# Attention and product-key feed-forward in float32 pairs, one core: GpSimd makes the odd v tile's low part beside dots

## The reference

```python
def block(xb):
    ...
    s_top, i_top = lax.top_k(s, PEER_TOPK)
    ...
    best, pos = lax.top_k(cand, PEER_TOPK)
    eidx = jnp.take_along_axis(cand_idx, pos, axis=-1)
    g = jax.nn.softmax(best, axis=-1)
    ug = jnp.take(u, eidx, axis=0)
    vg = jnp.take(v, eidx, axis=0)
    h = jax.nn.gelu(jnp.einsum('td,thkd->thk', xb, ug).astype(jnp.float32), approximate=False)
    return jnp.einsum('thk,thkd->td', (g * h).astype(x.dtype), vg)
```

## Time and profile before

| | |
|---|---|
| median of 3 runs | 1775.45 us (1773.05 to 1778.77) |
| the profiled execution, its own time | 1774.55 us |
| its span | 1772.4 us |
| mean granted TensorE clock | 0.983 |
| TensorE busy | 1700.3 us, 96% |
| VectorE busy | 1262.4 us, 71% |
| ScalarE busy | 639.2 us, 36% |
| GpSimd busy | 605.3 us, 34% |
| DMA | 422.76 MB, mean 239 GB/s |

### The profile page before, as it was taken

One profiled execution on the slowest core, in us unless ns is written; L12 is line 12 of the kernel. 1 busy time (PEld: TensorE's weight loads), 2 busy tenths in 40 slices (PEclk: granted clock), 3 DMA queues, 4 the chain that ended last, 5 costly groups with the idle time before them and its releaser, 6 DMA issues.

```text
span 1772.4 us, 23346 instructions
## 1 busy us (share of the span) xinstructions
PE 1700.3 (96%) x8969; PEld 1492.6 (84%) x8969; DVE 1262.4 (71%) x2325; ACT 639.2 (36%) x1011; POOL 605.3 (34%) x270
## 2 busy tenths in 40 slices
PE   8999998899979999999999999997999999999997
PEld 6898896677768899999999999996777777778775
DVE  1003345555259995998899999957888898888886
ACT  3213333443232234334344435432333343333333
POOL 4423221225353463444344433432232232322202
PEclk9999999999989999999999999998999999999999
DMA  5422101112312267777798999999999999999981
GB/s 190 172 81 72 48 24 50 48 60 83 143 48 96 84 179 276 240 246 280 255 335 323 333 345 335 348 365 376 373 376 372 380 376 377 367 382 379 385 278 60
DMA packets 144382, 422.76 MB, mean 239 GB/s; under 512 B 11152, under 2 KB 76944, under 8 KB 123024
## 3 DMA queue, kind: packets, MB, share of 16 engines
q1 hardware_dynamic: 125840, 287.05, 45.3%
q0 software_dynamic: 18432, 134.23, 20.2%
HBM read 368.80 MB, written 52.43 MB: 238 GB/s over the span
## 4 chain that ended last, share of the span: by engine, by line
PE 62%; DVE 24%; DMA 10%; issue 2%; ACT 1%; POOL 1%; SPq 0%; POOLq 0%; ACTq 0%; DVEq 0%
PE bank L1156 18%; PE bank L1157 18%; PE bank L1158 18%; DMA raw<-in_uv 7%; DVE acc L1066 6%; DVE wlo L1044 6%; DVE uvb L1052 4%; PE bank L1377 2%; DVE alo L1096 2%; DVE af L1089 2%; PE bank L1245 1%; PE bank L1212 1%; PE xpair L1260 1%; DMA gl<-g_scratch 1%; PE bank L1214 1%
## 5 line engine op out<-in xcount | busy, mean ns | idle before, releaser
L1156 PE MATMUL bank<-xhi,whi 128*128 128x384 f32 (+1 forms) x1440 | 516.2, 358 | 12.1 <-DVE xlo L796 8.5
L1157 PE MATMUL bank<-xlo,whi 128*128 128x384 f32 (+1 forms) x1440 | 509.4, 354 | 0.0
L1158 PE MATMUL bank<-xhi,wlo 128*128 128x384 f32 (+1 forms) x1440 | 508.9, 353 | 0.0
L539 POOL DMA_INDIRECT uvb<-in_uv,eidx x128 | 214.0, 1672 | 391.2 <-DVE acc L1066 371.0
L709 ACT ACTIVATE whi<-raw 128x1024 fp32r<-128x1024 f32 x256 | 270.0, 1055 | 207.6 <-DMA raw<-in_uv 135.4
L1156 PE MATMUL bank<-whi,ahi 128*128 128x512 f32 x768 | 305.9, 398 | 20.4 <-DVE alo L1096 20.4
L1157 PE MATMUL bank<-wlo,ahi 128*128 128x512 f32 x768 | 304.3, 396 | 0.0
L1158 PE MATMUL bank<-whi,alo 128*128 128x512 f32 x768 | 304.2, 396 | 0.0
L1156 PEld LDWEIGHTS bank<-xhi,whi 128*128 128x128 f32 x1440 | 273.5, 190 | 30.3 <-issue 12.0
L495 POOL TENSOR_TENSOR wlo<-raw,whi 128x2048 fp32r<-128x2048 f32 (+1 forms) x38 | 170.0, 4475 | 358.2 <-ACT whi L569 358.1
L1158 PEld LDWEIGHTS bank<-xhi,wlo 128*128 128x128 f32 x1440 | 273.2, 190 | 17.8
(11 more groups left out here) (191 smaller groups left out, 1870.6 us busy)
## 6 DMA issues: line engine op xcount, KB each, us to landing
raw<-in_u SPq DMA_DIRECT2D x128, 512.0 KB, 6.0
raw<-in_uv SPq DMA_DIRECT2D x128, 512.0 KB, 8.9
h_scratch<-hout SPq DMA_DIRECT2D x128, 192.0 KB, 6.3
g_scratch<-stage SPq DMA_DIRECT2D x48, 512.0 KB, 7.9
hl<-h_scratch SPq DMA_DIRECT2D x32, 768.0 KB, 10.3
gl<-g_scratch SPq DMA_DIRECT2D x32, 768.0 KB, 12.3
raw<-in_w_in SPq DMA_DIRECT2D x22, 1024.0 KB, 4.8
raw<-in_w_q SPq DMA_DIRECT2D x8, 1024.0 KB, 4.7
```

The lines of the kernel that those rows point to most:

```text
L539: nc.gpsimd.indirect_dma_start(out=uvb[:, k % UVB, :], out_offset=None, in_=a["uv"][:, :], in_offset=bass.IndirectOffsetOnAxis(ap=eidx[:, ...
L1156: mm(out, lh, rh, start=first, stop=False)
L1157: mm(out, lh, rl, start=False, stop=False)
L1158: return mm(out, ll, rh, start=False, stop=last)
```

## The change

In the 40 dot beats of the v stage the low part of the odd tile is made by GpSimd (line L553 of the new kernel), and VectorE leaves it out. GpSimd does not start when the high part is there but waits also until the second product of that beat is done (`a_done`, counted up by `product`), which in VectorE's order is the instruction before the first dot. The low parts of odd v tiles are now counted by two semaphores, one for GpSimd's and one for VectorE's, and `wait_low` chooses for TensorE and SyncE which to wait on. The wait of VectorE on GpSimd's count at tile 129 is dropped.

```diff
+def low_beside_dots(n):
+
+    return n % 2 == 1 and NT <= n < 2 * NT - 2 and n // 2 in SUM_BEATS
+
+
+def odd_lows(n):
+
+    pool = NT // 2 + sum(low_beside_dots(m) for m in range(NT + 1, n + 1, 2))
+    return pool, (n + 1) // 2 - pool
...
+        lo_odd = sem("lo_odd")
...
+        def wait_low(engine, n):
+
+            if n < NT or n % 2 == 0:
+                engine.wait_ge(tile_lo[n % 2], n // 2 + 1)
+            elif low_beside_dots(n):
+                engine.wait_ge(tile_lo[1], odd_lows(n)[0])
+            else:
+                engine.wait_ge(lo_odd, odd_lows(n)[1])
...
                 if n >= 4:
-                    sp.wait_ge(tile_lo[n % 2], (n - 4) // 2 + 1)
+                    wait_low(sp, n - 4)
...
             for n in range(2 * NT):
-                if n < POOL_ONLY or n < NT and n % 2 == 1:
+                if low_beside_dots(n):
+                    pool.wait_ge(a_done, n - NT + 3)
+                if n < POOL_ONLY or n < NT and n % 2 == 1 or low_beside_dots(n):
                     tile_low(n)
...
-                if n == NT + 1:
-                    dve.wait_ge(tile_lo[1], NT // 2)
                 V.tensor_tensor(wlo4[:, slot4(n), :], raw4[:, slot4(n), :], whi4[:, slot4(n), :].bitcast(F32),
-                                ALU.subtract).then_inc(tile_lo[n % 2], 1)
+                                ALU.subtract).then_inc(tile_lo[n % 2] if n < NT or n % 2 == 0 else lo_odd, 1)
...
                 tile_low(2 * beat)
-                if beat >= U_BEATS:
+                if beat >= U_BEATS and not low_beside_dots(2 * beat + 1):
                     tile_low(2 * beat + 1)
...
             for t in range(NT - 4):
-                pe.wait_ge(tile_lo[t % 2], (NT + t) // 2 + 1)
+                wait_low(pe, NT + t)
```

## The result

| | median us | range | runs | ratio to before [95% interval] |
|---|---|---|---|---|
| before | 1774.35 | 1773.05 to 1778.77 | 4 | |
| after | 1806.83 | 1804.14 to 1810.45 | 4 | 1.0177 [1.0153, 1.0201] |

The change costs 32 us. The forecast was a gain of 12: wrong, and the time lies outside the range. A ratio is estimated from the single runs and is not quite the quotient of the medians, here 1.0183. One run of the kernel before, of 1882.21 us at a granted clock of 0.842 where the others had 0.974 and more, is left out of every ratio.

A forecast was written before the change was run, and what follows sets the result against it. The v stage was taken as bound by a loop of raw load, ScalarE and VectorE; -1.1 - 2.0 - 9.5 = -12.6 us from 1774.55 gives 1762.0, plus 0.9 for the median: 1763, range 1758 to 1776.

The forecast's parts named there:

- What bounds the kernel: v stage: loop of raw load, ScalarE and VectorE, 51.6 us per six beats, falling to 49.0, below TensorE's 50.3.
- the 4 named as the sign of it: Sign the forecast is right: TensorE's waits on alo after the first total under 4 us.
- the 9.5 us that were priced as VectorE's time: v stage: TensorE stalls after the first pause won back by the shorter loop, 9.5 us taken from 0 to 13.
- Four gathers in a row: Rival, 12%, v stage: raw load waits behind four gathers, hl and gl; period 54.6 in half the periods, 1786 us.
- S + 9.7: Issue time of the next beat's even raw load, the one in the chain, 9.7 us after a dot beat's start S.
- The step on gathers: v stage: gathers queue behind GpSimd's new low part; 0 to 3 us of wait per three beats, taken as 0.
- a landing of 14.6: v stage: the critical raw load may take 14.6 us rather than 13.3 before TensorE stops setting the pace.
- The spacing: v stage: four gathers follow two lows, 2.17 us apart, from S + 5.7 to S + 14.4 of the second dot beat.
- The port: Dot beats: GpSimd's low sticks out past the dots and delays VectorE, 0.2 us per beat, ends 0 and 2.0.
- The start: Before the first v tile: one low fewer ahead, 1.1 us, and the gather of 1186.45 moved later, 2.0 us.
- The DMA engines: Rival, 17%: DMA bounds six beats at 51.3 us at 378 GB/s, so only the start is won, 1772.3 us.
- The port rival: Rival, 3%: lows start the dots late, sums pay 2.0 us instead of 0.2, loop 56.2 us, 1815 us.

The follow-up runs named there:

- e9: The change plus one wait: the second dot beat's gathers wait for the plain beat's products, so gathers leave late but in twos; 1762.17 us.
- e1: The change with GpSimd issuing a dot beat's two gathers ahead of the next dot beat's low part, not behind it; 1761.59 us.
- e7: The kernel before, all low parts on VectorE, with gathers held until the dots and the second pair until the plain beat's products; 1768.01 us.
- e6: e1 without the wait on a_done, so GpSimd makes the low part as soon as the high part is there; 1764.49 us.
- e2: The kernel before, no low part moved, with GpSimd waiting for each dot beat's dots before going on to the gathers; 1810.92 us.
- e8: e1 with the last two gathers of the u stage held until the first product of the v stage is done; 1761.99 us.
- e5: The change without its wait on a_done, gathers still behind the low part; 1798.41 us.

## Why the prediction was wrong

**What bounds the kernel: the loop right, its price not shown.** The raw load, then ScalarE, then VectorE's queue was the loop of the kernel before. With the gathers apart the time came out near the forecast of 1763: e9, which is the change and one wait, took 1762.17, and e1 1761.59. In e9 TensorE's later waits on alo were 3.2 us (8.7 - 5.5), under the 4 named as the sign of it, and the chain ran through TensorE's lines; in e1 they were 5.4. But e7, with every low part on VectorE, was already 7.5 us below before (1775.54 - 1768.01), and its ratio, 0.9956, cannot be told from that of e9, 0.9945. And e6 was faster than before with VectorE busier, 97% of this stretch instead of 87% (before, then e6):

```profile
1450.00:1700.00 250.00, 245.73 (x1051) 197.25 (x1050) 218.18 (x311) 89.18 (x138) 69.70 (x37) 1.00 1.01 377
1450.00:1700.00 250.00, 249.52 (x1066) 199.74 (x1066) 243.49 (x297) 90.30 (x137) 107.77 (x57) 1.00 1.01 375
```

So no run shows the 9.5 us that were priced as VectorE's time. The new spacing of the gathers can be the larger part of the gain of 12, and that the fast kernels lie at the forecast is partly luck.

**The step that failed** stands under "Four gathers in a row": "the load issued at S + 9.7 lands at S + 22.9, a landing of 13.2, as today". It took the 6.81 MB ahead of that load and divided by 396 GB/s, the rate of full engines. But the rate does not say who is served, and the engines were not full: they stood at a share of 0.49 for 8 us while four gathers were held, and the bytes that they did not move then had to pass later. The held low part ended at 1514.53 (1512.12 + 2.41) and the load of 1522.05 landed at 1538.15, 23.6 us behind it, where the step had 17.2. That load took 16.10 us, beyond the 15.9 from which that rival was said to decide. The step on gathers priced the crowd at 0 to 3 us of VectorE's waits for gathers; those came to 4.5 us in the whole stage. The price was paid by another: the raw loads in the other queue.

**The rival named the mechanism and sized it at half.** 1786 was worked out from one long load per 51.6 us, a period of 54.6 in half of the periods. The chain shows about two long loads, because each of the two pairs of dot beats in six beats sends its four, and the eight periods measured all took over 54 us, 55.1 on the mean. And no term was there for the clock, which gave 11 us after longer pauses. Its chance, 12%, was also too low: the rows of order already showed two low parts followed by four gathers through the whole stage. The slack of 1.4 us between a landing of 14.6 and one of 13.2 was the only thing between forecast and rival, and 13.2 was an assumption.

**The spacing was wrong.** Four gathers 2.17 us apart were assumed, from 1495.93 and 1498.10, though the gather of 1186.45 there took 0.94 us to issue; three of the four took 0.95 to 1.02, so they left 1.3 apart and the crowd was denser. What makes a gather take 0.95 or 1.9 us to issue was not tried.

**The port: priced at 0.2 per dot beat, measured 0.** The low part of 1488.93 ended at 1491.35, just ahead of the small product, whose mean from 1206 to 1700 us stayed at 161 ns, so the 0.3 us named as a sign did not come; the sums stayed at 1285 ns each. The order and place of the low part were as predicted.

**The start: right.** Forecast 1.1 + 2.0 us off the first pause of 9.6; after has 7.0, 2.6 less. In e2, where no low part moved but the gather of 1186.45 came later too, it was 7.5, so 2.1 us go with the gather. In e6, where again a third gather left among the first loads, it was 9.1, and in e8, with the last two gathers held as well, 1.8. Kernels with the same two gathers ahead of the loads had 5.3 to 7.5, so none of these is exact.

**The other rivals.** The DMA engines are no bound at 378 GB/s: e1 and e8 moved 389 over 460 us. The port rival did not come in the change; without the hold it did, in e5 and at alo in e6.

**Left open.** Whether the 8 us of idle engines ahead of the fours or the crowd behind them costs more: no kernel here had the one without the other.

## What to carry to other kernels

A compute step put ahead of DMA issues in an in-order queue is also a gate on them: ask not only whether they come in time, but in what groups they leave, and whose transfers they meet. A mean rate says nothing about the landing of one load; look at what the queues hold in the 10 us after its issue. Where pauses of TensorE grow from 1 us to 2 or more, price the clock with them as a risk. And a forecast that a repaired kernel then meets is not yet shown: a control with the repair and without the change (e7 here) can be almost as fast.

## What the runs showed that was not expected

- Holding four gathers together instead of two and two costs 43 to 45 us (e7 against e2, e9 against the change), with the same bytes and the same instructions.
- TensorE's clock fell after some short pauses of its work and not after others: after one of 1.79 us (ended 1487.59) the next stretch of 4 us stayed at 1.00, after one of 1.81 (ended 1653.20) it had 0.71, and after one of 3.64 the 8 us that followed had 0.68 and 0.89. The length alone does not decide: in e5 the 4 us behind pauses of 2.94 (ended 1544.41) and 3.26 us (ended 1599.26) were at 1.00, while behind one of 2.70 (ended 1270.38) they had 0.61.
- VectorE could be blocked for 82.5 us by GpSimd's low parts (e6) without a loss that the runs can tell; its idle time fell by 78.5.
- One core sustained 389 GB/s for 460 us, more than the 378 that looked like a limit before.
